# Seven block products for eight in a decoder step's merge columns, with x sums, gates and one input by way of device memory

## What is computed

```python
    (c_q, c_kv, k_r, z_mla, conv_b, conv_c, conv_h, z_conv,
     q_x, z_x, gates) = jnp.split(h @ w_in, SPLIT_POINTS, axis=-1)
...
    g = jax.nn.sigmoid(gates.astype(jnp.float32)).astype(h.dtype).reshape(b, s, N_BRANCH, d)
    m = (g[:, :, 0] * ((y_mla * jax.nn.silu(z_mla)) @ w_p_mla)
         + g[:, :, 1] * ((y_conv * jax.nn.silu(z_conv)) @ w_p_conv)
         + g[:, :, 2] * ((y_x * jax.nn.silu(z_x)) @ w_p_x))
    return _layer_norm(DEEPNORM_ALPHA * h + m @ w_o, ln_g, ln_b)
```

## Time and profile before

| | |
|---|---|
| median of 3 runs | 1538.75 us |
| span of the profiled execution, first to last instruction | 1441.9 us |
| outside that span (1538.75 - 1441.9) | 96.9 us |
| TensorE busy | 1404.6 us, 97% of the span, 10616 matmuls |
| VectorE, ScalarE, GpSimd busy | 49%, 28%, 30% |
| merge on TensorE, w_in and projections | 625.0 to 1336.9 us |
| output projection on TensorE | to 1434 us |

### The profile page before, as it was taken

How to read it: one execution, slowest core, us unless ns; L and a number is a source line. 1 busy time by engine, 2 the same in 40 slices (tenths; PEclk the granted TensorE clock), 3 DMA queues, 4 the chain that set the end, 5 groups by cost and what they waited for, 6 DMA issues and landing times.

```text
span 1441.9 us, 26631 instructions
## 1 busy us (share of the span) xinstructions
PE 1404.6 (97%) x10616; PEld 1258.3 (87%) x10616; DVE 709.0 (49%) x1426; ACT 401.4 (28%) x990; POOL 433.0 (30%) x326
## 2 busy tenths in 40 slices
PE   7999999999989999999999999999999999999997
PEld 7998977777756676689999999999999999999885
DVE  3251356776777876435443522237333372029645
ACT  4321456665353333321111111112111121114100
POOL 3110037765544553022222222222222222227000
PEclk9999999999999999999999999999999999999999
DMA  6361020001474787941111111111211111113622
GB/s 224 99 262 36 0 89 1 1 1 32 135 258 153 236 288 236 354 109 45 44 45 45 45 44 45 45 45 47 55 45 45 44 45 45 45 44 103 249 88 73
DMA packets 111983, 138.62 MB, mean 96 GB/s; under 512 B 13714, under 2 KB 81106, under 8 KB 111860
## 3 DMA queue, kind: packets, MB, share of 16 engines
q1 hardware_dynamic: 101620, 101.27, 22.5%
q0 software_dynamic: 10240, 35.66, 7.3%
HBM read 120.66 MB, written 16.23 MB: 95 GB/s over the span
## 4 chain that ended last, share of the span: by engine, by line
PE 56%; DVE 0%; issue 0%; ACT 0%; DVEq 0%
PE ps L2103 49%; PE ps L2137 6%; PE ps L2124 0%; DVE p_h L2367 0%; DVE p_h L2370 0%; DVE p_stats L2354 0%; DVE p_h L2350 0%; PE ps L2114 0%; DVE p_mv L2361 0%; ACT p_rt L2183 0%; DVE p_stats L2359 0%; DVE p_rs L2365 0%; DVE p_stats L2358 0%; DVE p_ve L2363 0%; DVEq L2348 0%
## 5 line engine op out<-in xcount | busy, mean ns | idle before, releaser
L2103 PE MATMUL ps<-p_xh,p_wh 128*128 128x352 f32 (+1 forms) x1152 | 376.3, 327 | 0.7 <-PEq L1791 0.7
L2103 PE MATMUL ps<-p_xh,p_wl 128*128 128x352 f32 (+1 forms) x1152 | 376.4, 327 | 0.0
L2103 PE MATMUL ps<-p_xl,p_wh 128*128 128x352 f32 (+1 forms) x1152 | 376.3, 327 | 0.0
L2191 POOL TENSOR_TENSOR p_wl<-p_wr,p_wh 128x512 fp32r<-128x512 f32 x118 | 165.0, 1414 | 515.4 <-DVE p_wh L2209 515.4
L2103 PEld LDWEIGHTS ps<-p_xh,p_wh 128*128 128x128 f32 x1152 | 216.3, 188 | 0.9 <-issue 0.9
L2103 PEld LDWEIGHTS ps<-p_xh,p_wl 128*128 128x128 f32 x1152 | 216.2, 188 | 0.0
L2103 PEld LDWEIGHTS ps<-p_xl,p_wh 128*128 128x128 f32 x1152 | 216.2, 188 | 0.0
L2209 DVE CAST p_wh<-p_wr 128x512 fp32r<-128x512 f32 x118 | 47.3, 436 | 335.9 <-ACT p_stage L2176 246.9
L2176 ACT ACTIVATE p_stage<-ps 128x384 f32<-128x384 f32 x168 | 79.4, 473 | 365.7 <-PE ps L2103 365.7
L904 POOL TENSOR_SCALAR p_pr<-p_pr,p_rec 128x896 f32<-128x896 f32 (+3 forms) x64 | 109.6, 1722 | 143.1 <-DVE p_rec L868 143.0
L2103 PE MATMUL ps<-p_uh,p_wh 128*128 128x352 f32 (+1 forms) x288 | 94.4, 328 | 0.0
(11 more groups left out here) (315 smaller groups left out, 2493.8 us busy)
## 6 DMA issues: line engine op xcount, KB each, us to landing
p_wr<-w_in SPq DMA_DIRECT2D x104, 256.0 KB, 2.9
x_kept<-p_xh SPq DMA_DIRECT2D x8, 544.0 KB, 6.5
x_kept<-p_xl SPq DMA_DIRECT2D x8, 544.0 KB, 6.7
p_xh<-x_kept SPq DMA_DIRECT2D x8, 544.0 KB, 6.2
p_xl<-x_kept SPq DMA_DIRECT2D x8, 544.0 KB, 5.8
p_xs<-x_prompt SPq DMA_DIRECT2D x8, 512.0 KB, 3.9
p_wr<-w_o SPq DMA_DIRECT2D x16, 256.0 KB, 2.8
p_x<-x_prompt SPq DMA_DIRECT2D x8, 512.0 KB, 3.7
```

The source lines that it names most:

```text
L2103: last = pe.matmul(ps[:, g % 8, 0:tn], w[:, v % HL, kt % UK, :], x[:, kt, t0:t0 + tn], start=(kt == 0 and q == 0), stop=(kt == nk - 1 and ...
L2191: nc.gpsimd.tensor_tensor(wl[:, v % HL], wr[:, v % RAW], f32(wh[:, v % HL]), ALU.subtract).then_inc(wl_done, 1)
```

## The change

One level of Strassen's scheme (in Winograd's form) for w_in's merge columns. x (in turned form) is cut in four blocks: two halves of the contraction, and two interleaved halves of T (PW = 272 rows, twice). w_in is taken in groups of 256 columns, again four blocks. 7 products of sums of blocks replace 8 products of blocks. 24 groups x 7 products x (2 x 4 x 3) matmuls of 272 columns.

- **x sums.** The four sums of x blocks (T1 to T4) are made in the first stage: VectorE in 16 parts (`make`), ScalarE rounds (`high`), VectorE takes the low part (`lower`), SyncE stores (`t_store`), through four buffers. The three plain blocks are stored as well (`b_store`).
- **Loads.** The 14 half blocks are 1088 KB each; 9 come in decode_attention, 5 in cross_decode. GpSimd clears the used semaphores once more, at the start of cross_prompt.
- **Weights.** 3 raw buffers of 512 KB, four weight sums per group on VectorE (`w_sum`), rounding on ScalarE (`w_high`), low parts of w_in on VectorE (`lower`), of the projections' weights on GpSimd (`w_low`); 3 slots.
- **Chains.** Products add up in PSUM in three chains of two banks; ScalarE keeps three intermediate sums (`keep`), VectorE adds them (`add`), ScalarE the fourth block (`last_block`).
- **Gates and u.** Gates are stored to device memory and loaded again for the projections; so is the convolution branch's u. All of w_in's columns come first, then the three branches' projections.
- **w_o** is split in 128x1024 parts, each pair behind a weight of the last projections on GpSimd.

The diff, cut. First the first stage: a part's four steps on VectorE and where the parts stand (behind latent tile i; more follow between the norms), ScalarE's roundings behind piece g of q_x, and SyncE's stores:

```diff
+            def make(n):
...
+                dve.wait_ge(xl_done, NT if pp else 5)
+                if again:
+                    dve.wait_ge(t_out[z], 32 * again)
+                dve.tensor_tensor(f[:, :, :].rearrange("p (k h) w -> p k h w", k=2), by_block(xh), by_block(xl), ALU.add
+                                  ).then_inc(t_step, 1)
+                dve.tensor_tensor(f[:, 0:2, :], f[:, 1:4:2, :], f[:, 0:2, :], ALU.subtract).then_inc(t_step, 1)
...
+                dve.tensor_tensor(f[:, 3, :], f[:, 3, :], f[:, 0, :], ALU.subtract).then_inc(t_step, 1)
...
+                dve.tensor_tensor(f[:, 2, :], f[:, 2, :], f[:, 3, :], ALU.subtract).then_inc(t_step, 1)
...
+            def next_part(n):
+                make(n)
+                if n > NGR // 2:
+                    lower(n - 1)
...
+                if i >= 5:
+                    for n in (2 * (i - 5), 2 * (i - 5) + 1):
+                        make(n)
+                    for n in (2 * (i - 5), 2 * (i - 5) + 1):
+                        lower(n)
...
                     last.then_inc(qx_kept, 1)
+                    if g < NGR // 2:
+                        high(NGR // 2 + g)
...
+            for n in range(4, NGR):
+                t_store(n)
+                if n - 2 < 12:
+                    b_store(n - 2)
+            sp.wait_ge(x_stored, 16 * 12)
+            for z in range(2, SETS):
+                sp.wait_ge(t_out[z], 32 * NGR // 4)
```

The loads, in decode_attention and on SyncE in cross_decode:

```diff
-X_EARLY = [(0, t) for t in range(3, KT)] + [(1, t) for t in range(KT - 1)] + [(0, t) for t in range(3)]
+X_EARLY = [(B11, 0), (B11, 1), (T1, 0), (T1, 1), (T2, 0), (T2, 1), (B21, 0), (B21, 1), (T3, 0)]
...
+            load_x(sp, k, e, T3, 1)
+            for n in range(2):
+                sp.wait_ge(o_done, KV_EARLY + n + 1)
+                load_raw(sp, a, e, groups, n)
+            for blk, part in ((B22, 0), (B22, 1), (T4, 1)):
+                load_x(sp, k, e, blk, part)
+            sp.wait_ge(cc_turned, 1)
+            load_x(sp, k, e, T4, 0)
```

The merge, in this order: TensorE; ScalarE; VectorE; GpSimd; ScalarE in the last eight projections (d counts them from 0):

```diff
+            def product(g, i):
+                q = NPROD * g + i
...
+                pe.wait_ge(w_hi, q + 1)
+                pe.wait_ge(w_lo, q + 1)
+                for z in range(2):
+                    for t in range(KH):
+                        for n, (part, v) in enumerate(((0, xh), (0, xl), (1, xh))):
+                            last = pe.matmul(ps[:, lo + z, 0:PW], w[:, q % NW, part, t, :], v[:, t, z * PW:(z + 1) * PW],
...
+            for g in range(NGRP):
+                for i in range(NPROD):
+                    q = NPROD * g + i
+                    act.wait_ge(prod_done, q + 1)
+                    if i < 3:
+                        keep(g, i)
+                    elif i > 3:
+                        sigmoid(g, i - 4)
+                    if i == A22:
+                        last_block(g)
+                    w_high(nc, act, e, q + NW)
...
+            for g in range(NGRP):
+                q = NPROD * g + NW
+                if g:
+                    finish(g - 1, 2)
+                    lower(q + A22 - NPROD)
+                    finish(g - 1, 3)
+                w_sum(dve, e, g, S3)
+                if kinds[g] == "b":
+                    convolve(g, 0)
+                lower(q + A11)
+                w_sum(dve, e, g, S4)
+                lower(q + S1)
+                if kinds[g] == "b":
+                    convolve(g, 1)
+                lower(q + S2)
+                add(g, 0)
+                lower(q + A12)
+                add(g, 1)
+                lower(q + S3)
+                if g + 1 < NGRP:
+                    w_sum(dve, e, g + 1, S1)
+                finish(g, 0)
+                add(g, 2)
+                lower(q + S4)
+                if g + 1 < NGRP:
+                    w_sum(dve, e, g + 1, S2)
+                finish(g, 1)
+            for j in range(4):
+                u_low(0, j)
...
+            for q in (*range(1, NW), *range(NQ1, NQ)):
+                w_low(nc, pool, e, q)
+                if NQ - 6 <= q < NQ - 2:
+                    for t in range(2):
+                        w_o_low(2 * (q - NQ + 6) + t)
...
+                if p >= 2 * KT:
...
+                    if 1 <= d < 4:
+                        w_o_high(2 * d)
+                        w_o_high(2 * d + 1)
+                if p + NW < NJ:
+                    act.wait_ge(piece_done, NP * (p + 1))
+                    w_high(nc, act, e, NQ1 + p + NW)
```

More of the change, by code:

```diff
@@ L56 @@
 NP = len(PIECES)
+PW = T // 4
+KH = KT // 2
+B11, T1, T3, T4, T2, B21, B22 = range(7)
+GW = PW // 2
 def rows(i):
@@ L1383, in _ @@
             mid = list(range(KV_EARLY, KV_EARLY + KV_MID))
-            for part, t in X_EARLY:
-                if mid and late["x_free"](part, t) > NG - LAG:
+            for blk, part in X_EARLY:
+                if mid and late["x_free"](blk, part) > NG - LAG:
                     sp.wait_ge(scored, NG // S)
@@ L2002, in merge @@
     assert t.at <= k["y_at"]
-    pieces = [(n, i) for n in range(len(jobs)) for i in range(NP)]
-    staged_before, s_count = [], 0
-    for n, i in pieces:
-        staged_before.append(s_count)
-        s_count += 0 if jobs[n][:2] == ("gate", 0) else 2 if jobs[n][0] == "z" else 1
-    NU, NPC = len(units), len(pieces)
-    TAIL = next(g for g, (n, _) in enumerate(pieces) if jobs[n][:2] == ("proj", 0))
-    WO = 2 * KT
+    u_src = [k["y_x"], k["y_mla"], u1]
+    kinds = [g[0] for g in groups]
@@ new lines, in merge, with banks, sums, tile_half @@
+    GATES = kinds.index("gate")
+    n_slots = {"c": 0, "h": 1, "b": 1, "z": 2, "gate": 0}
+    slot0 = [4 * sum(n_slots[kind] for kind in kinds[:g]) for g in range(NGRP)]
+    USED = slot0[GATES]
+    CHAIN = (0, 1, 0, 2, 0, 1, 0)
+    STARTS = (A11, S1, A12)
+    def banks(g, chain):
+        lo = (2 * (g % 2), 4, 6)[chain]
+        return slice(lo, lo + 2)
+    def sums(g, chain):
+        return ps[:, banks(g, chain), 0:PW]
+    def tile_half(o):
+        return ((0, 0), (1, 1), (0, 1), (1, 0))[o]
@@ new lines, in wait_gates, with dest, wait_dest @@
+        def wait_gates(eng, places):
+            for z in places:
+                eng.wait_ge(g_out[z], 16 * sum(s % RST == z for s in range(4 * (NGRP - GATES))))
+        def dest(g, o, second=0):
+            tile, half = tile_half(o)
+            if kinds[g] == "c":
+                return cols(co[:, tile, :], half)
+            return slots[:, slot_of(g, o, second) % RST]
+        def wait_dest(eng, g, o):
+            if kinds[g] == "c":
+                if groups[g][2]:
+                    eng.wait_ge(u_out[tile_half(o)[0]], 16)
+            else:
+                wait_slot(eng, g, o)
@@ L2047, in _ @@
+            for t in range(2, KT):
+                load_w_o(t)
             sp.wait_ge(piece_done, NPC)
@@ L2122, in _ @@
                     for t in range(KT):
-                        for part, cols in two:
-                            last = pe.matmul(ps[part, 2 * (i % 2), :], m_last[:, t, :], w_o[:, t, cols],
+                        for part, half in two:
+                            last = pe.matmul(ps[part, 2 * (i % 2), :], m_last[:, t, :], w_o[:, t, half],
                                              start=(t == 0), stop=(t == KT - 1), tile_position=(0, part.start))
@@ L2224, in _, with add @@
-            for g, (n, i) in enumerate(pieces):
-                kind, br, j, _ = jobs[n]
-                (t0, tn), s = PIECES[i], staged_before[g]
-                pn = min(tn, SEQ - t0)
-                if g >= TAIL:
-                    dve.wait_ge(freed, g)
-                    dve.wait_ge(piece_done, g + 1)
-                    if i == NP - 1:
-                        w_hi_until(sum(1 for v in range(NU) if v < HL or units[v - HL][0] <= n))
-                    z = stage[:, s % ST, 0:tn]
-                    if g == TAIL:
-                        dve.wait_ge(used, s)
-                    if g >= TAIL + ST:
+            def add(g, o):
+                chain, i, part = ((2, A12, 0), (0, S3, 1), (1, S4, 2))[o]
+                dve.wait_ge(prod_done, NPROD * g + i + 1)
+                dve.wait_ge(kept[part], g + 1)
+                wait_dest(dve, g, o)
+                dve.tensor_tensor(dest(g, o), sums(g, chain), temp[part][:, :, :], ALU.add).then_inc(added[o], 1)
@@ L2242, in _ @@
+                    if n == 0:
+                        dve.wait_ge(summed, NP * (d + 1))
+                    dve.tensor_tensor(z, z, dst, ALU.add).then_inc(zed, 1)
                     if g > TAIL:
                         m_low(g - 1)
[L2244 to L2249 removed]
```

893 lines of the change are left out of this document (597 added, 296 removed).

## The result

The changed kernel takes **1520.86 us** (median of 4, 1518.72 to 1521.78) where the kernel before, measured beside it, takes 1539.38 us: a ratio of 0.9876, 95% interval [0.9862, 0.9890], 18.5 us faster. The prediction had 1484.9 us, 53.9 us faster, with a range of 1470 to 1517.

The account below looks back on a forecast made before the run. TensorE was taken to bound the kernel from 625 us on. -71.2 (product) + 6 (first stage) + 5.8 (caches) + 1 + 1 + 3.5 = -53.9 on a 1441.9 us span, plus 96.9 around it, gives 1484.9 us; range 1470 to 1517.

Parts of the forecast that it names:

- What bounds the kernel: From 625.02 us on, TensorE's matmuls alone end the chain, so each one removed saves its full start-to-start distance.
- the caches: Before the merge: 2.8 MB more x loads delay the memory keys and values; 5.8 us of TensorE waiting, ends 0 and 8.
- the b groups: Two w_in groups with two added convolutions nearly fill VectorE; priced at 1 us together, 0 to 5.
- The product itself: w_in's 3456 matmuls, 569.6 us, become 4032 of 272 columns at 123.6 ns, 498.4 us: 71.2 us less.
- no fixed cost is seen down to 288: Matmul time taken as proportional to columns, from first-stage distances of 0.13 and 0.31 us; hence 123.6 ns at 272 columns.
- The first stage: Sixteen x sums of 2.6 us VectorE work and their stores start the second stage 6 us later, ends 0 and 12.
- 89.6 + 6.2 + 18.6 + 20.8: First stage's end: latent norms' start, their delay, the old work behind, eight sums of 2.6 us; 135 us.
- Every store waited for in turn: High end of the first-stage term: 12 us later instead of 6.
- The projections: After w_in: 1 us for the first projection's input low parts, 3.5 us for w_o's low parts delaying last projections.
- The 96.9 us: Gap between the profiled span of 1441.9 us and the median of 1538.75, taken as untouched by any edit.
- start and tail: After w_in: the first projection's input, 1 us (0 to 4), and the last projections beside w_o, 3.5 us (0 to 8).
- the rivals: Additions hide, 1467.6 us, chance 0.1; hand-offs leak, 1509, 0.2; matmul floor, 1515, 0.05; waits before every product, 1629, 0.07.

Follow-up runs that it names:

- e2_v123: Changed kernel with the low part ahead of the next x sum and two changes of order behind w_in: 1402.72 us, kernel before 1443.46.
- e1_after: Changed kernel, unchanged, timed again: 1521.88 us, kernel before 1539.04 in that batch.
- e2_after: Changed kernel, unchanged, timed again in a quick batch: 1423.09 us, kernel before 1443.46.
- e3_pieces4: Kernel before with output pieces cut to four of 272 columns instead of 384, 352 and 352: 1552.56 us, kernel before 1540.57.
- e0_before: Kernel before, unchanged, profiled again: 1442.90 us, kernel before 1443.41 in that batch.

## Why the prediction was wrong

**What bounds the kernel** was right: no wait in w_in's part, and its gain reached the end. Right as well were the caches (5.1 us of waiting predicted as 5.8, and 2.7 of it went when 1.1 MB was moved behind them), the b groups (no wait at all), and that VectorE keeps up with 24 groups.

**The product itself, -71.2 us, was mis-sized by 7.9.** The step that failed is "no fixed cost is seen down to 288". The earlier trace rows give distances rounded to 0.01 us; with 8 ns besides 0.432 ns a column, 288 columns would take 132 ns and the pair of 384 and 288 some 306, and by proportionality 131 and 305; the row's 0.13 and 0.31 can't tell these apart. Two distances, read to 10 ns, were taken to exclude a fixed part of 8. The rule of the Trainium skill that stands beside it there (page "TensorE: Matmul & The Clock Gate", section "Back-to-back issue gap") gave an estimate of 64 us saved, and 63.3 were measured. Its form, a fixed part for every matmul, fits these runs where my reading of the rows did not; that the savings agree so closely is luck, since both of its figures are lower than the line's (2.5 ns for 8, and 1/2.4 = 0.417 ns a column for 0.432), which for one matmul makes 115.8 ns for the measured 125.6 and in the saving nearly cancels.

**The first stage, +6 us, was the largest miss: +21.9.** The step that failed is the sum "89.6 + 6.2 + 18.6 + 20.8". It charged eight sums of the second half at their work, 2.6 us each, while in the first half it counted the landing of a store before a buffer is used again. That wait stands in the second half too, behind a low part which the program places after the next sum. The norms of the latents began at 97.9 us, 8.3 later than in the earlier trace rows where 6.2 were predicted; from the third sum behind them on, the sums came 6 to 8 us apart. With that order undone the turn came at 141.0 us, where the prediction had it near 140. "Every store waited for in turn" was named as the term's high end, and priced at 12 us: the end was worth 22.

**The projections, +4.5 us, were +14.7.** The two places were named rightly and priced low: 2.8 us for the first input's low parts (1 predicted), 5.7 for weights behind w_o's low parts (3.5). (The profile names no releaser for the 5.7; for 3.3 of the 5.3 us in e2_v123 it names GpSimd's low part of a weight.) Some 6 us more were not in the sum at all: TensorE's granted clock was below full behind the first input's waits, 0.68 from 1165 to 1173 us, and behind the last wait for a weight, 0.83 from 1300 to 1310, and the matmuls after 1165 us stand 0.29 us apart, not 0.16. Not every wait did this: from 1284 to 1300 us, with two waits of 0.6 and 2.5 us, the clock stayed at 1.00. A wait of TensorE was charged at its own length. And the slow operations of the earlier trace rows were counted as VectorE's pace but not followed to their cause, GpSimd's part of w_o: with that part on VectorE, ScalarE's roundings reordered and the first input's low parts one addition earlier, 13.3 us of the 14.7 are gone.

**The 96.9 us** were put "around the span", which no trace had shown. They were lost between the second stage's start and the merge, in the decode stage above all, in batches of the slow kind. That made no difference to the forecast's change, but the sentence was a guess in the form of a sum: with 1.8 us around a span of 1520.0 the trace and the times of before could not have been of like runs.

**The range** failed by 3.9 us, since two of its ends (12 for the first stage, 12 for start and tail together) were below what came (21.9 and 14.7). None of the rivals happened: TensorE did not wait per group or per product. The cost lay in the stages around the product, as in the forecast, at 42.7 us instead of 16.3 (17.3 with the b groups' 1).

## What to carry to other kernels

Price a buffer that is stored and used again by its whole cycle (work, the place of the last operation in the program, issue, landing), in every part of a stage, not by its work; and look whether the operation that releases the store can go ahead of the one that waits for it, which here gave back 15 of 22 us with one line moved. Charge a wait of TensorE at its length, and reckon with a lower clock behind it: here 8.5 us of waits in the projections came with some 6 us more. And when VectorE is the pace, an operation taken over from GpSimd may cost it less than the same operation left beside it: in the 44 us shown of the last projections the stalls of two-input operations came to (2104 - 526) x 9 + (1987 - 558) x 5 ns = 21 us beside GpSimd's eight pieces of w_o and to (912 - 526) x 14 = 5 us without them, 2 us for a piece that VectorE makes in 1.2.

## What the runs showed of the hardware

VectorE beside a busy GpSimd is not slower in general. A 128x352 or 128x544 operation with both inputs in SBUF went from 0.53 to as much as 2.7 us, or from 719 to 1265 ns in the mean; one with an input in PSUM kept its 516 or 724 ns, and so did two-input ones that met no operation of GpSimd (526 ns). The Trainium skill's page "SBUF — State Buffer", section "SBUF: two separate sides", says that a VectorE operation with two SBUF inputs and a GpSimd operation that reads SBUF take a shared pair of ports in turns, each for its whole instruction; the traces agree, with stalls of up to 2.2 us beside GpSimd's operations of 2.5.

The decode stage has two paces for the same program, 1879 or 1029 matmuls in 100 us. In the slow one TensorE waits 22 to 28 us, in 40 to 47 pieces, for nothing that the trace shows, in front of the 32-row matmuls of line 1546, where the quick one has 1.7 us; first e1_after, then e2_after:

```profile
PE ps L1546 <- issue: 27.8, 45, 2.7
```

```profile
PE ps L1546 <- issue: 1.7, 1, 1.7
```

The clock is low behind these waits. Four us of e3_pieces4, columns as in the earlier trace rows: TensorE is busy 0.79 of 2 us at a granted clock of 1.00, and 0.52 is granted in the next 2.

```profile
464.00:466.00 2.00, 0.79 (x2) 0.26 (x2) 0.71 (x2) 0.00 (x0) 1.11 (x2) 1.00 0.96 353
466.00:468.00 2.00, 1.54 (x32) 1.54 (x39) 0.00 (x0) 0.00 (x0) 0.00 (x0) 0.52 0.72 273
```

The DMA is 0.96 busy while TensorE waits, and 0.11 and 0.03 busy from 468 to 472 us, when TensorE works on. That speaks for waits for the pages' loads, which then come in bursts, but the quick trace e0_before has the DMA at 0.98 to 1.03 from 454 to 458 us with TensorE busy throughout. What makes the difference from one batch to the next stays open; no run here tells it, and the chip does not decide it.
